# The convolutions of a state-space mixer: the first tap on ScalarE, and the engines' steps set one unit apart

## The chip, the cores and the metric

The kernel runs on one core of one Trainium2 chip. The metric is the device time of an execution in microseconds (us). TensorE (PE) multiplies, VectorE (DVE) and ScalarE (ACT) work element by element, GpSimd (POOL) helps them, and SyncE (SP) issues the loads of the weights. The engines run side by side and meet at semaphores.

## The reference, cut to what matters

Three layers work on x (256 tokens, 1024 features): attention and a gated feed-forward, a spatial gating unit and a gated feed-forward, and a third block whose mixer is half state-space scan, half attention. The change lies in that mixer's projections:

```python
proj = rmsnorm(x, norm_mix_pre) @ w_in              # z, xbc, dt, q, k, v
def depthwise_conv_centred(u, w, b):                # five taps over the tokens, 1536 channels
    out = conv(u, w, padding=[(2, 2)], feature_group_count=c)
    return out + b
xbc = silu(depthwise_conv_centred(xbc, conv_w, conv_b))
xs, B, C = split(xbc)                               # 1024, 256 and 256 channels
dt = softplus(dt_raw + dt_bias)                     # then the chunked scan, forwards and backwards
```

## The kernel before, in words

All weights come in units of 128 x 1024 fp32, in the order of their use, through a ring of six places (`RING`). For each unit n, SP loads `raw`, ScalarE writes the high half (`hi_of`, L144: a copy rounded to fp32r), VectorE the low half (`lo_of`, L149: raw minus high), and TensorE makes three products for each piece (`three`, L166 to L168): high by high, high by low, low by high. The high half of n waits until TensorE has used unit n-6, the load of n+6 until VectorE has split n. `hi_to` and `lo_to` split all units up to a number that haven't been split yet; where they stand in an engine's program is where the engine does it. Each engine takes its own instructions strictly in the written order.

The mixer's projections run in 12 steps j (`XT`), written out by hand for each engine. Unit `x_unit(j)` holds 128 channels of xbc; for j below 10 (`QKT`) the unit behind it holds 128 channels of q or k; steps 10 and 11 have the first unit alone. The result has channels on partitions and tokens along the row, so a convolution is five shifted multiply-adds along the row.

TensorE (`mixer_in_pe`, L1187): 24 matmuls of the x unit into bank 4 or 5, in turn; the two transposes of channel block j-1 (`turn`, L1193), which wait for its Silu; the 24 matmuls of the query or key unit into bank 2 or 3, which wait until VectorE has emptied that bank of block j-2. In step 0 it also makes the row of the norm and the transposes of dt, and waits for VectorE's copy of the row; in step 8 it makes the sums of dt (L1316).

VectorE (`mixer_in_dve`, L1248): the low splits up to `x_unit(j) + 5`; the copy of the x unit's result into `pad`, scaled by the row (L1263); the first tap with its bias (L1267, `tensor_scalar`); four more taps (L1271, `scalar_tensor_tensor`, each waits for the one before); in steps 0 and 1 small operations of dt; the low split of `x_unit(j) + 6`; the query or key of the same step (L1281).

ScalarE (`mixer_in_act`, L1225): the high split up to `x_unit(j) + 5`; the copy of the transposed block j-2 out of PSUM (`move`, L1229); the high split of `x_unit(j) + 6`; the Silu of block j (L1245), which waits for its last tap. In step 0 it works on dt between these (Exp, a table load, Ln, a table load for Silu). Behind the loop it loads the table of Exp and makes the decays (L1330).

`pad` and `S_CV` (the running sum) have two places each, used in turn. Behind the loop comes the scan (`ssd_pe`, `ssd_act`, `ssd_dve`, `ssd_pool`). TensorE enters it once move 9, copy 11 and the last key are done. POOL makes masks for it (L1399), two ahead at first and then as TensorE uses them. VectorE's first product for it (L1514, `decayed`) waits for the decays, and ScalarE's exponentials for Silu 11.

Of the kernel before, what the change touches and what calls it, by code (L numbers as in the profile page):

```python
# [9 lines left out]
ACT = mybir.ActivationFunctionType  # L10
ALU = mybir.AluOpType
# [3 lines left out]
SEQ = 256  # L15
# [5 lines left out]
HEADS, KV_HEADS, DH = 16, 4, 64  # L21
REP = HEADS // KV_HEADS
QT = HEADS * DH // P
KVT = KV_HEADS * DH // P
QKT = QT + KVT
# [9 lines left out]
XT = 1536 // P  # L35
# [29 lines left out]
C_XBC = C_CONV + 2 * FT * 4  # L65
# [14 lines left out]
def build(nc, w, x_in, cols_in, misc_in, tables_in, rows_in, ws_in, wdt_in, out):  # L80
# [3 lines left out]
    def sem(name):  # L84
        return nc.alloc_semaphore(name)

    def signals(prefix, names):

        return namedtuple(prefix, names)(*(sem(f"{prefix}_{name}") for name in names.split()))
# [9 lines left out]
    cols = sb("cols", [P, COLS])  # L99
# [7 lines left out]
    pad = sb("pad", [P, 2, SEQ + 4])  # L107
    arena = sb("arena", [P, 16640])
    ps = nc.alloc_psum_tensor("ps", [P, 8, 512], F32)
# [19 lines left out]
    unit_used = sem("unit_used")  # L129
# [29 lines left out]
    def lo_to(dve, n):  # L159
        while dve_at[0] <= min(n, UNITS - 1):  # L160
            lo_of(dve, dve_at[0])
            dve_at[0] += 1
# [59 lines left out]
    ROW = cut(16384, SEQ)  # L222
# [361 lines left out]
    A_Q, A_K, A_V = cut(3072, QT, SEQ), cut(5120, KVT, SEQ), cut(5632, TT, KV_HEADS * DH)  # L584
# [585 lines left out]
    S_E, S_LA, S_CB = cut(12288, 4, 512), cut(14336, 2, 512), cut(15360, 2, 2, P)  # L1170
    S_CV, S_SL = cut(12288, 2, SEQ), cut(12800, 2, SEQ)
    S_Z = cut(12288, TT, D)
    x_sem = signals("xbc", "copied conv silu turned moved")

    def xbc_dst(j):
        return S_SL[:, j % 2, :] if j < 8 else S_F[:, j - 8, :]


    def x_unit(j):
        return N_MIX + 2 + (2 * j if j < QKT else j + QKT)  # L1180

    def x_bank(j):
        return 4 + j % 2
# [3 lines left out]
    def mixer_in_pe(pe, u, q):  # L1187
        def turn(j):
            pe.wait_ge(x_sem.silu, j + 1)
            if j >= 2:  # L1190
                pe.wait_ge(x_sem.moved, j - 1)
            for tt in range(TT):
                mm = pe.transpose(ps[:, 6 + j % 2, tt * P:(tt + 1) * P],  # L1193
                                  xbc_dst(j)[:, tt * P:(tt + 1) * P], ident)
            mm.then_inc(x_sem.turned, 1)

        def v(tt, pre):
            for h in range(2):
                tokens(pe, N_MIX + h, [ps[:, b, 0:256] for b in V_BANKS], 4 * h, 4, 256, pre=pre, tiles=(tt,))

        v(0, Pre(u.next.lo, 2 * KT * u.n))
        turn_tile_pe(pe, u, 1)
        v(1, after(u))
        dt_pe(pe)
        for j in range(XT):
            if j >= 2:
                pe.wait_ge(x_sem.copied, j - 1)
            features(pe, x_unit(j), ps[:, x_bank(j), 0:SEQ])
            if j == 0:
                row_pe(pe, u, 2)  # L1210
                dt_turn_pe(pe)
            if 1 <= j < XT - 1:
                turn(j - 1)
            if j == DT_SUMS:
                dt_sums_pe(pe)
            if j < QKT:
                if j == 0:
                    pe.wait_ge(next_sems.row_out, 4)
                elif j == 1:
                    pe.wait_ge(q.v, TT)  # L1220
                else:
                    pe.wait_ge(q.qk, j - 1)
                features(pe, x_unit(j) + 1, ps[:, 2 + j % 2, 0:SEQ])

    def mixer_in_act(act):  # L1225
        def move(j):
            act.wait_ge(x_sem.turned, j + 1)
            dst = S_X[:, :, j * P:(j + 1) * P] if j < 8 else S_B[:, :, (j - 8) * P:(j - 7) * P]
            act.activation(dst, ps[:, 6 + j % 2, 0:SEQ].rearrange("p (a b) -> p a b", a=TT),  # L1229
                           ACT.Copy).then_inc(x_sem.moved, 1)  # L1230

        for j in range(XT):
            if j == 0:
                dt_move_act(act)
            hi_to(act, x_unit(j) + 5)
            if 2 <= j < XT:
                move(j - 2)
            hi_to(act, x_unit(j) + 6)
            if j == 0:
                dt_act(act)  # L1240
                act.preload_act_table(ACT.Silu)
            act.wait_ge(x_sem.conv, 5 * j + 5)
            if 2 <= j < 8:
                act.wait_ge(x_sem.turned, j - 1)
            act.activation(xbc_dst(j), S_CV[:, j % 2, :], ACT.Silu).then_inc(x_sem.silu, 1)  # L1245
        decay_act(act)

    def mixer_in_dve(dve, q, u):  # L1248
        dve.wait_ge(next_sems.inv, TT * (u.n + 1))
        for tt in range(TT):  # L1250
            dve.wait_ge(unit_used, N_MIX + 2)
            dve.tensor_scalar(A_V[:, tt, :], ps[:, V_BANKS[tt], 0:256], st[:, 14 + tt:15 + tt], None,
                              ALU.mult).then_inc(q.v, 1)
        dt_before, dt_between, dt_behind = dt_dve(dve)
        for j in range(XT):
            lo_to(dve, x_unit(j) + 5)
            if j == 0:
                row_dve(dve, 4, 2)
                dt_before()
            c = C_XBC + 6 * j  # L1260
            b = j % 2
            dve.wait_ge(unit_used, x_unit(j) + 1)
            dve.tensor_tensor(pad[:, b, 2:2 + SEQ], ps[:, x_bank(j), 0:SEQ], ROW, ALU.mult).then_inc(x_sem.copied, 1)  # L1263
            dve.wait_ge(x_sem.copied, j + 1)
            if j >= 2:
                dve.wait_ge(x_sem.silu, j - 1)
            dve.tensor_scalar(S_CV[:, b, :], pad[:, b, 0:SEQ], cols[:, c:c + 1], cols[:, c + 5:c + 6],  # L1267
                              ALU.mult, ALU.add).then_inc(x_sem.conv, 1)
            for k in range(1, 5):
                dve.wait_ge(x_sem.conv, 5 * j + k)  # L1270
                dve.scalar_tensor_tensor(S_CV[:, b, :], pad[:, b, k:k + SEQ], cols[:, c + k:c + k + 1],  # L1271
                                         S_CV[:, b, :], ALU.mult, ALU.add).then_inc(x_sem.conv, 1)
            if j == 0:
                dt_between()
            if j == 1:
                dt_behind()
            lo_to(dve, x_unit(j) + 6)
            if j < QKT:
                dve.wait_ge(unit_used, x_unit(j) + 2)
                dst = A_Q[:, j, :] if j < QT else A_K[:, j - QT, :]  # L1280
                dve.scalar_tensor_tensor(dst, ps[:, 2 + j % 2, 0:SEQ], DH ** -0.5 if j < QT else 1.0, ROW,  # L1281
                                         ALU.mult, ALU.mult).then_inc(q.qk, 1)


    dts = sb("dts", [P, 12, 64])
# [46 lines left out]
    def dt_dve(dve):  # L1332


        v = lambda k: dts[:, k, :]
        two = lambda k: v(k).rearrange("p (a b) -> p a b", a=TT)
        row32 = lambda t, o: t[:, o:o + 32].rearrange("p (a b) -> p a b", a=1).to_broadcast([P, TT, 32])
        step = [0]

        def then(ins):  # L1340
            ins.then_inc(d_sem.step, 1)
            step[0] += 1
            dve.wait_ge(d_sem.step, step[0])

        def before():
            dve.wait_ge(d_sem.turned, 1)
            for tt in range(TT):
                then(dve.scalar_tensor_tensor(two(V_A)[:, tt, :], ps[:, 1, SEQ + 32 * tt:SEQ + 32 * (tt + 1)],
                                              st[:, 14 + tt:15 + tt], misc[:, M_DTB:M_DTB + 32], ALU.mult, ALU.add))
            then(dve.scalar_tensor_tensor(v(V_NEG), v(V_A), -1.0, v(V_A), ALU.mult, ALU.min))  # L1350

        def between():
            dve.wait_ge(d_sem.exp, 2)
            then(dve.tensor_scalar(v(V_U), v(V_E), 1.0, None, ALU.add))
            then(dve.tensor_scalar(v(V_D), v(V_U), 1.0, None, ALU.subtract))
            then(dve.tensor_scalar(v(V_EQ), v(V_U), 1.0, None, ALU.is_equal))
            then(dve.tensor_tensor(v(V_D2), v(V_D), v(V_EQ), ALU.add))
            then(dve.reciprocal(v(V_RD), v(V_D2)))
            then(dve.tensor_tensor(v(V_T), v(V_E), v(V_RD), ALU.mult))

        def behind():
            dve.wait_ge(d_sem.ln, 1)
            then(dve.tensor_tensor(v(V_D), v(V_L), v(V_EQ), ALU.add))
            then(dve.tensor_tensor(v(V_T), v(V_T), v(V_D), ALU.mult))
            then(dve.scalar_tensor_tensor(v(V_DT), v(V_A), 0.0, v(V_T), ALU.max, ALU.add))
            then(dve.scalar_tensor_tensor(two(V_DA), two(V_DT), -1.0, row32(ea, 0), ALU.mult, ALU.mult))

        return before, between, behind
# [381 lines left out]
    first, mix = Norm(0, *pre_sems), Norm(1, *pre_sems)  # L1750
# [264 lines left out]
```

## Time and profile before

| | us |
|---|---|
| median of 3 runs | 1149.39 (1148.82 to 1149.48) |
| the profiled execution | 1150.9 |
| its span, first to last instruction | 1149.1 |
| TensorE busy in it | 1088.8 (95%) |
| VectorE busy | 818.2 (71%) |
| ScalarE busy | 609.1 (53%) |
| POOL busy | 128.2 (11%) |
| mean granted clock of TensorE | 0.986 |

The profile is of one execution, and its times are counted from its first instruction. Matmuls are pipelined, so a busy TensorE is not one at its peak. The granted clock is a share of 2.4 GHz. The loop of the mixer's projections lies between about 721 and 800 us of the span, the scan behind it until about 850.

### The profile page before, as it was taken

The numbers are of one execution on the slowest core, as the hardware profiler recorded it, in microseconds if no ns is written. First come the engines' busy times: TensorE is split into PE (matmuls) and PEld (weight loads), VectorE is DVE, ScalarE is ACT, GpSimd is POOL, SyncE is SP. The second block draws the span as 40 slices with busy tenths as digits, with TensorE's granted clock in tenths as the row PEclk, the third lists the DMA queues.
The fourth block names the chain that finished last, engine by engine and source line by source line (L and its number), as shares of the span: only waits on it lengthen the run. The fifth ranks groups of instructions, "written<-read, shape, count | busy, mean of one in ns | idle before, by whom it ended". The sixth has DMA issues, their size and how long they took to land.

```text
span 1149.1 us, 20549 instructions
## 1 busy us (share of the span) xinstructions
PE 1088.8 (95%) x7226; PEld 983.5 (86%) x7226; DVE 818.2 (71%) x1282; ACT 609.1 (53%) x1046; POOL 128.2 (11%) x139
## 2 busy tenths in 40 slices
PE   7989999999999999999999999897788898999997
PEld 7878999999788997779999998897666687999996
DVE  6757877776744567878777776899878658666664
ACT  6657444444755846656444446544337746444442
POOL 0140111111010012201111110101402200000000
PEclk9999999999999999999999999899899999999999
DMA  8253665565455555435656563554001273655540
GB/s 331 95 190 133 216 194 189 189 195 183 163 204 165 191 177 175 155 111 165 201 183 198 185 201 110 184 183 148 1 1 37 93 229 119 201 185 190 190 147 37
DMA packets 51381, 185.08 MB, mean 161 GB/s; under 512 B 5728, under 2 KB 6240, under 8 KB 51328
## 3 DMA queue, kind: packets, MB, share of 16 engines
q1 hardware_dynamic: 49248, 178.28, 47.2%
q0 software_dynamic: 1504, 5.44, 1.4%
q8 instruction: 35, 0.57, 0.2%
q10 hardware_dynamic: 576, 0.64, 0.2%
q14 instruction: 18, 0.15, 0.0%
HBM read 183.28 MB, written 1.05 MB: 160 GB/s over the span
## 4 chain that ended last, share of the span: by engine, by line
PE 85%; DVE 9%; ACT 4%; issue 2%; DMA 0%; DVEq 0%; SPq 0%; ACTq 0%
PE ps L208 26%; PE ps L166 17%; PE ps L167 17%; PE ps L168 17%; DVE w_lo L149 2%; DVE arena L1534 1%; PE ps L645 1%; PE ps L674 1%; ACT arena L698 1%; DVE a_lo L382 1%; DVE x L400 1%; PE ps L658 1%; DVE arena L393 1%; ACT a_hi L376 1%; PE ps L1444 1%
## 5 line engine op out<-in xcount | busy, mean ns | idle before, releaser
L149 DVE TENSOR_TENSOR w_lo<-raw,w_hi 128x1024 fp32r<-128x1024 f32 x336 | 420.9, 1262 | 140.5 <-ACT w_hi L144 140.3
L144 ACT ACTIVATE w_hi<-raw 128x1024 fp32r<-128x1024 f32 x336 | 347.1, 1052 | 174.1 <-PE ps L168 106.7
L166 PE MATMUL ps<-a_hi,w_hi 128*128 128x256 f32 x1408 | 401.6, 285 | 3.4 <-DVE arena L354 3.0
L167 PE MATMUL ps<-a_lo,w_hi 128*128 128x256 f32 x1408 | 399.6, 284 | 0.0
L168 PE MATMUL ps<-a_hi,w_lo 128*128 128x256 f32 x1408 | 399.5, 284 | 0.0
L166 PEld LDWEIGHTS ps<-a_hi,w_hi 128*128 128x128 f32 x1408 | 271.2, 193 | 7.7 <-DVE arena L354 3.1
L167 PEld LDWEIGHTS ps<-a_lo,w_hi 128*128 128x128 f32 x1408 | 271.3, 193 | 2.5
L168 PEld LDWEIGHTS ps<-a_hi,w_lo 128*128 128x128 f32 x1408 | 271.2, 193 | 0.0
L208 PE MATMUL ps<-w_hi,a_hi 128*128 128x512 f32 x496 | 158.1, 400 | 8.3 <-DVE a_lo L1116 3.0
L208 PE MATMUL ps<-w_lo,a_hi 128*128 128x512 f32 x496 | 153.5, 390 | 0.0
L208 PE MATMUL ps<-w_hi,a_lo 128*128 128x512 f32 x496 | 153.3, 390 | 0.0
L208 PEld LDWEIGHTS ps<-w_lo,a_hi 128*128 128x128 f32 x496 | 93.1, 188 | 20.6
L208 PEld LDWEIGHTS ps<-w_hi,a_lo 128*128 128x128 f32 x496 | 93.1, 188 | 20.1
L208 PEld LDWEIGHTS ps<-w_hi,a_hi 128*128 128x128 f32 x496 | 86.0, 190 | 24.8 <-DVE w_lo L149 4.5
L524 POOL TENSOR_TENSOR arena<-arena 128x256 f32<-128x256 f32 x44 | 47.1, 1070 | 308.8 <-ACT arena L511 308.8
L511 ACT ACTIVATE arena<-arena 128x256 f32<-128x256 f32 x44 | 18.4, 419 | 101.8 <-DVE arena L551 101.8
L166 PE MATMUL ps<-w_hi,a_hi 128*128 128x512 f32 (+1 forms) x160 | 60.6, 379 | 0.0
L516 ACT ACTIVATE a_hi<-arena 128x256 fp32r<-128x256 f32 x44 | 18.4, 418 | 77.9 <-DVE arena L557 77.9
L167 PE MATMUL ps<-w_lo,a_hi 128*128 128x512 f32 (+1 forms) x160 | 59.0, 369 | 0.0
L168 PE MATMUL ps<-w_hi,a_lo 128*128 128x512 f32 (+1 forms) x160 | 58.9, 368 | 0.0
L551 DVE SCALAR_TENSOR_TENSOR arena<-pad,cols,arena 128x256 f32<-128x256 f32 x88 | 42.7, 485 | 10.2 <-DVE arena L547 0.3
L166 PEld LDWEIGHTS ps<-w_hi,a_hi 128*128 128x128 f32 x160 | 30.1, 188 | 7.6 <-issue 2.2
(183 smaller groups left out, 1064.6 us busy)
## 6 DMA issues: line engine op xcount, KB each, us to landing
raw<-in_w SPq DMA_DIRECT2D x336, 512.0 KB, 4.2
row<-in_rows POOLq DMA_DIRECT2D x7, 512.0 KB, 4.0
x<-in_x SPq DMA_DIRECT2D x2, 512.0 KB, 4.8
out<-x SPq DMA_DIRECT2D x4, 256.0 KB, 2.0
misc<-in_misc POOLq DMA_DIRECT2D x1, 512.0 KB, 6.1
arena<-in_ws POOLq DMA_DIRECT2D x1, 512.0 KB, 7.5
tab<-in_tables POOLq DMA_DIRECT2D x1, 320.0 KB, 4.8
tab<-in_tables POOLq DMA_DIRECT2D x1, 256.0 KB, 5.1
```

The costliest lines, as they stand in the source:

```text
L144: act.activation(w_hi[:, s, :], raw[:, s, :], ACT.Copy).then_inc(hi_done, 1)
L149: dve.tensor_tensor(w_lo[:, s, :], raw[:, s, :], w_hi[:, s, :].bitcast(F32), ALU.subtract).then_inc(lo_done, 1)
L166: pe.matmul(o, l_hi, r_hi, start=first, stop=False)
L167: pe.matmul(o, l_hi, r_lo, start=False, stop=False)
L168: return pe.matmul(o, l_lo, r_hi, start=False, stop=last)
L208: mm = pe.matmul(ps[:, 2 * tt + c, :], a[:, slot, t], b[:, s, c * 512:(c + 1) * 512], start=f, stop=z)
L376: act.activation(a_hi[:, k, tile(tt)], spun(tt, k), ACT.Copy, scale=gain(g, k)).then_inc(u.next.hi, 1)
L382: dve.scalar_tensor_tensor(a_lo[:, k, tile(tt)], spun(tt, k), gain(g, k), a_hi[:, k, tile(tt)].bitcast(F32), ALU.mult, ALU.subtract).then_ ...
L511: act.activation(F_GL[:, b, :], F_CV[:, b, :], ACT.Gelu_apprx_tanh).then_inc(f.gelu, 1)
L516: act.activation(a_hi[:, f_slot(t), :], F_PR[:, b, :], ACT.Copy).then_inc(f.hi, 1)
L524: pool.tensor_tensor(F_GR[:, b, :], F_GL[:, b, :], ROW, ALU.mult).then_inc(f.scaled, 1)
L551: dve.scalar_tensor_tensor(F_CV[:, b, :], pad[:, b, k:k + SEQ], col(k), F_CV[:, b, :], ALU.mult, ALU.add).then_inc(f.conv, 1)
```

## The change

VectorE's first tap with its bias becomes an Identity activation on ScalarE (`first_tap`), with the tap's column as scale and the bias column as bias. It waits for VectorE's copy and for the Silu that last read its place. VectorE's taps wait for it.

The order of all three programs moves. TensorE's transposes of block j-2 (was j-1) stand in step j. ScalarE does in step j: the high split of `x_unit(j) + 5`, move j-3 (was j-2), the first tap of j, the high split of `x_unit(j) + 6`, and the Silu of j-1 (was j); move 9 and Silu 11 stand behind the loop. VectorE does in step j: the low split of `x_unit(j) + 5`, the copy of j (with two more waits, on the taps and the first tap that read this place of `pad`), the low split of `x_unit(j) + 6`, the query or key of j-1 (was j, at the end), the four taps of j, and then the small operations of dt in steps 0 and 1.

```diff
--- before.py
+++ after.py
@@ -1170,7 +1170,7 @@
     S_E, S_LA, S_CB = cut(12288, 4, 512), cut(14336, 2, 512), cut(15360, 2, 2, P)
     S_CV, S_SL = cut(12288, 2, SEQ), cut(12800, 2, SEQ)
     S_Z = cut(12288, TT, D)
-    x_sem = signals("xbc", "copied conv silu turned moved")
+    x_sem = signals("xbc", "copied first conv silu turned moved")
 
     def xbc_dst(j):
         return S_SL[:, j % 2, :] if j < 8 else S_F[:, j - 8, :]
@@ -1209,8 +1209,8 @@
             if j == 0:
                 row_pe(pe, u, 2)
                 dt_turn_pe(pe)
-            if 1 <= j < XT - 1:
-                turn(j - 1)
+            if 2 <= j < XT:
+                turn(j - 2)
             if j == DT_SUMS:
                 dt_sums_pe(pe)
             if j < QKT:
@@ -1229,20 +1229,35 @@
             act.activation(dst, ps[:, 6 + j % 2, 0:SEQ].rearrange("p (a b) -> p a b", a=TT),
                            ACT.Copy).then_inc(x_sem.moved, 1)
 
+        def first_tap(j):
+            c = C_XBC + 6 * j
+            act.wait_ge(x_sem.copied, j + 1)
+            if j >= 2:
+                act.wait_ge(x_sem.silu, j - 1)
+            act.activation(S_CV[:, j % 2, :], pad[:, j % 2, 0:SEQ], ACT.Identity, bias=cols[:, c + 5:c + 6],
+                           scale=cols[:, c:c + 1]).then_inc(x_sem.first, 1)
+
+        def silu(j):
+            act.wait_ge(x_sem.conv, 4 * j + 4)
+            if 2 <= j < 8:
+                act.wait_ge(x_sem.turned, j - 1)
+            act.activation(xbc_dst(j), S_CV[:, j % 2, :], ACT.Silu).then_inc(x_sem.silu, 1)
+
         for j in range(XT):
             if j == 0:
                 dt_move_act(act)
             hi_to(act, x_unit(j) + 5)
-            if 2 <= j < XT:
-                move(j - 2)
+            if 3 <= j < XT:
+                move(j - 3)
+            first_tap(j)
             hi_to(act, x_unit(j) + 6)
             if j == 0:
                 dt_act(act)
                 act.preload_act_table(ACT.Silu)
-            act.wait_ge(x_sem.conv, 5 * j + 5)
-            if 2 <= j < 8:
-                act.wait_ge(x_sem.turned, j - 1)
-            act.activation(xbc_dst(j), S_CV[:, j % 2, :], ACT.Silu).then_inc(x_sem.silu, 1)
+            else:
+                silu(j - 1)
+        move(XT - 3)
+        silu(XT - 1)
         decay_act(act)
 
     def mixer_in_dve(dve, q, u):
@@ -1251,6 +1266,12 @@
             dve.wait_ge(unit_used, N_MIX + 2)
             dve.tensor_scalar(A_V[:, tt, :], ps[:, V_BANKS[tt], 0:256], st[:, 14 + tt:15 + tt], None,
                               ALU.mult).then_inc(q.v, 1)
+        def query(j):
+            dve.wait_ge(unit_used, x_unit(j) + 2)
+            dst = A_Q[:, j, :] if j < QT else A_K[:, j - QT, :]
+            dve.scalar_tensor_tensor(dst, ps[:, 2 + j % 2, 0:SEQ], DH ** -0.5 if j < QT else 1.0, ROW,
+                                     ALU.mult, ALU.mult).then_inc(q.qk, 1)
+
         dt_before, dt_between, dt_behind = dt_dve(dve)
         for j in range(XT):
             lo_to(dve, x_unit(j) + 5)
@@ -1260,26 +1281,23 @@
             c = C_XBC + 6 * j
             b = j % 2
             dve.wait_ge(unit_used, x_unit(j) + 1)
+            if j >= 2:
+                dve.wait_ge(x_sem.conv, 4 * j - 4)
+                dve.wait_ge(x_sem.first, j - 1)
             dve.tensor_tensor(pad[:, b, 2:2 + SEQ], ps[:, x_bank(j), 0:SEQ], ROW, ALU.mult).then_inc(x_sem.copied, 1)
-            dve.wait_ge(x_sem.copied, j + 1)
-            if j >= 2:
-                dve.wait_ge(x_sem.silu, j - 1)
-            dve.tensor_scalar(S_CV[:, b, :], pad[:, b, 0:SEQ], cols[:, c:c + 1], cols[:, c + 5:c + 6],
-                              ALU.mult, ALU.add).then_inc(x_sem.conv, 1)
+            lo_to(dve, x_unit(j) + 6)
+            if 1 <= j <= QKT:
+                query(j - 1)
+            dve.wait_ge(x_sem.first, j + 1)
             for k in range(1, 5):
-                dve.wait_ge(x_sem.conv, 5 * j + k)
+                if k > 1:
+                    dve.wait_ge(x_sem.conv, 4 * j + k - 1)
                 dve.scalar_tensor_tensor(S_CV[:, b, :], pad[:, b, k:k + SEQ], cols[:, c + k:c + k + 1],
                                          S_CV[:, b, :], ALU.mult, ALU.add).then_inc(x_sem.conv, 1)
             if j == 0:
                 dt_between()
             if j == 1:
                 dt_behind()
-            lo_to(dve, x_unit(j) + 6)
-            if j < QKT:
-                dve.wait_ge(unit_used, x_unit(j) + 2)
-                dst = A_Q[:, j, :] if j < QT else A_K[:, j - QT, :]
-                dve.scalar_tensor_tensor(dst, ps[:, 2 + j % 2, 0:SEQ], DH ** -0.5 if j < QT else 1.0, ROW,
-                                         ALU.mult, ALU.mult).then_inc(q.qk, 1)
 
 
     dts = sb("dts", [P, 12, 64])
```

## Rows read from the trace of the kernel before

**Rows 1.** Stretch table: busy us and instructions by engine, TensorE's clock, DMA share, GB/s

```profile
772.00:778.00 6.00, 6.00 (x52) 6.00 (x51) 5.45 (x9) 2.70 (x4) 0.00 (x0) 1.00 0.54 176
```

**Rows 2.** Timeline of TensorE in the loop: start us, us, engine, line, operation

```profile
784.88 0.38 PE L1193 MATMUL ps<-tab,arena 128*128 128x128 f32 x2
...
790.85 0.38 PE L1193 MATMUL ps<-tab,arena 128*128 128x128 f32 x2
```

**Rows 3.** Timeline of VectorE, one step of the loop and the next low split

```profile
785.08 0.42 DVE L1263 TENSOR_TENSOR pad<-ps,arena 128x256 f32<-128x256 f32 x1 [0.50 <-PE ps L168]
785.54 0.41 DVE L1267 TENSOR_SCALAR arena<-pad,cols 128x256 f32<-128x256 f32 x1
785.99 2.05 DVE L1271 SCALAR_TENSOR_TENSOR arena<-pad,cols,arena 128x256 f32<-128x256 f32 x4
787.96 1.22 DVE L149 TENSOR_TENSOR w_lo<-raw,w_hi 128x1024 fp32r<-128x1024 f32 x1
789.09 0.42 DVE L1281 SCALAR_TENSOR_TENSOR arena<-ps,arena 128x256 f32<-128x256 f32 x1
789.47 1.22 DVE L149 TENSOR_TENSOR w_lo<-raw,w_hi 128x1024 fp32r<-128x1024 f32 x1
...
793.92 1.22 DVE L149 TENSOR_TENSOR w_lo<-raw,w_hi 128x1024 fp32r<-128x1024 f32 x1
```

**Rows 4.** Timeline of TensorE at the start: in brackets the idle before

```profile
727.71 0.58 PE L166 MATMUL ps<-a_hi,w_hi 128*128 128x256 f32 x1 [2.98 <-DVE arena L354]
```

**Rows 5.** Stretch table, behind that wait

```profile
728.00:736.00 8.00, 8.00 (x47) 8.00 (x47) 7.41 (x17) 4.57 (x7) 0.00 (x0) 0.64 0.44 168
```

**Rows 6.** Timeline of VectorE at the end of the loop

```profile
795.06 0.42 DVE L1263 TENSOR_TENSOR pad<-ps,arena 128x256 f32<-128x256 f32 x1
...
795.96 3.55 DVE L1271 SCALAR_TENSOR_TENSOR arena<-pad,cols,arena 128x256 f32<-128x256 f32 x4
...
801.53 0.17 DVE L1514 TENSOR_TENSOR decayed<-dts,ex 128x8 f32<-128x8 f32 x1
```

**Rows 7.** Groups of ScalarE by form: count, busy us, mean ns, idle before

```profile
L144 ACT ACTIVATE w_hi<-raw 128x1024 fp32r<-128x1024 f32 x336 | 347.1, 1052 | 174.1 <-PE ps L168 106.7 <-PE ps L208 64.3 <-DMA raw<-in_w 2.7
...
L1015 ACT ACTIVATE arena<-arena,lns 128x128 f32 x36 | 15.6, 480 | 0.0
```

**Rows 8.** Timeline of ScalarE: start of the loop, and one later step

```profile
728.91 1.28 ACT L1324 ACT_TABLE_LOAD   x1
...
788.07 0.42 ACT L1245 ACTIVATE arena<-arena 128x256 f32<-128x256 f32 x1 [1.87 <-DVE arena L1271]
788.39 1.04 ACT L144 ACTIVATE w_hi<-raw 128x1024 fp32r<-128x1024 f32 x1
789.35 0.36 ACT L1229 ACTIVATE arena<-ps 128x256 f32<-128x256 f32 x1
```

**Rows 9.** Timeline of VectorE in the first two steps

```profile
728.52 0.42 DVE L1263 TENSOR_TENSOR pad<-ps,arena 128x256 f32<-128x256 f32 x1
...
731.39 0.19 DVE L1354 TENSOR_SCALAR dts<-dts 128x64 f32<-128x64 f32 x1
...
736.39 0.43 DVE L1263 TENSOR_TENSOR pad<-ps,arena 128x256 f32<-128x256 f32 x1 [0.52 <-PE ps L168]
...
739.26 0.22 DVE L1363 TENSOR_TENSOR dts<-dts 128x64 f32<-128x64 f32 x1
...
740.29 1.23 DVE L149 TENSOR_TENSOR w_lo<-raw,w_hi 128x1024 fp32r<-128x1024 f32 x1
```

**Rows 10.** Timelines of TensorE and POOL at the start of the scan

```profile
795.57 0.46 PE L1424 MATMUL ps<-arena 128*128 128x128 f32 x2 [1.47 <-ACT arena L1229]
...
797.01 2.22 POOL L1399 TENSOR_TENSOR arena<-tab,dts 128x512 f32<-128x512 f32 x2 [52.61 <-PE ps L1414]
```

**Rows 11.** Stretch table, in the spatial gating unit

```profile
432.00:440.00 8.00, 6.58 (x35) 5.43 (x33) 5.18 (x7) 5.95 (x12) 0.92 (x2) 1.00 0.73 238
```

## The prediction

> **What bounds the kernel now.** I read the stretch table first, then the timelines of VectorE, TensorE and ScalarE in the loop of the mixer convolutions, then the same timelines at its end. From 772 to 778 us TensorE is busy 6.00 of 6.00 us while VectorE has 5.45 and ScalarE 2.70 [rows 1]. So in the loop TensorE sets the pace: its two transposes of a step recur after 790.85 - 784.88 = 5.97 us [rows 2]. A step is 48 matmuls and these transposes.
>
> VectorE is only just faster. From start to next start [rows 3]: copy 0.46, first tap 0.45 (785.54 to 785.99), four taps 1.97 (785.99 to 787.96), low split 1.13 (787.96 to 789.09), query 0.38 (789.09 to 789.47), second low split 1.14 (793.92 to 795.06). The sum is 5.53 us, 0.44 under TensorE's 5.97. The copy at 785.08 waited 0.50 us for a matmul [rows 3]: VectorE is ready before its work is.
>
> Two places are not TensorE's. At the start it waits 2.98 us for the row copied by VectorE and then runs at a granted clock of 0.64 over 728 to 736 us, mostly the lower level of 1.2 GHz [rows 4, 5]; the change leaves what is in front of this wait alone. At the end the chain runs through VectorE: copy 11 at 795.06, taps until 795.96 + 3.55 = 799.51, then Silu, a table load and the decays on ScalarE, and VectorE's decayed at 801.53 [rows 6]. The state product of the scan waits for that.
>
> **The change, part by part.** *Removed from VectorE:* twelve first taps, 0.45 us of its order each, 5.4 us in all. In the loop they lie beside TensorE's work and are worth nothing there; only the last is on the path, 0.45.
>
> *Added to ScalarE:* twelve Identity activations of 128x256 with a column for scale and one for bias. The nearest row is Identity with two such columns on 128x128, 0.480 us. A plain activation takes 0.42 for 256 elements and 1.052 for 1024, so 128 more cost (1.052 - 0.42) / 6 = 0.105; I take 0.585 [rows 7, 8]. Bounds: 0.42, the plain one of the same size, and 0.70, both columns dearer on the longer tile. ScalarE is busy 2.70 of 6 us [rows 1], so as work this is free. The Trainium skill ("ScalarE: Activation LUTs", rules for kernel authors) says to keep multiplies and adds on VectorE; the comparison here, 0.585 against 0.41, agrees, and by busy time alone the rule would cost nothing in this loop.
>
> *The new exchange* is what costs. In a step VectorE now does the copy, then the low split of unit x+6, the lagging query, the taps, and the low split of the next x+5. But that low split of x+6 needs ScalarE's high split of x+6, and ScalarE issues it behind first tap j, which waits for VectorE's copy j. Before, VectorE ran five taps between copy and split (0.45 + 1.97 = 2.42 us), long enough for ScalarE to have the split ready. Now nothing stands there. From the copy's start to the low split's start:
> - the copy 0.42, and 0.03 until ScalarE starts (taps end 785.99 + 2.05 = 788.04, Silu starts 788.07): 0.45 [rows 3, 8]
> - first tap 0.585, of which the next activation overlaps 0.10 (788.07 + 0.42 against 788.39): 0.49 [rows 8]
> - high split 1.052 and 0.03 back to VectorE: 1.08 [rows 7]
>
> together 2.02 us, of which VectorE works 0.42. Then low split 1.13, query 0.38, taps 1.97, low split 1.14: 4.62. The step closes on itself because the engine takes its instructions in order: 6.64 us, against TensorE's 5.97. The first tap gone saves 0.45; the idle 1.56 more than eats it.
>
> *When TensorE feels it.* The unit of query j waits for query j-2 to leave its bank, and that query now stands one step later. It is done 2.02 + 1.13 + 0.42 + 0.03 = 3.6 us after the copy of its step. The start uses up the slack:
> - copy 0 stays at 728.52 [rows 9]. ScalarE's tap and high split end at 730.54, low split to 731.67, taps to 733.64, the first dt operation 0.19 later [rows 9]. Only then can ScalarE do its Ln (about 0.3, as the Exps) and load Silu's table (1.28 [rows 8]): 735.4. Its next high split is done at 736.5, VectorE's low split at 737.6: copy 1 at 737.6 instead of 736.39 [rows 9].
> - copy 2 one ring later plus the last dt operations, 740.29 - 739.26 = 1.03 [rows 9]: 737.6 + 6.64 + 1.03 = 745.3. Query 1 is out at 748.9. TensorE, done with x unit 1 at 736.4 (copy 1 of before waited for it), would be done with x unit 3 at 736.4 + 2 x 5.97 = 748.3 and want that bank. It pauses 0.5 us, and from here about 6.64 - 5.97 = 0.67 us in each step.
> - copies 3 to 10: 8 x 6.64 = 53.1, so copy 10 at 798.4. Copy 11 has no low split in front: 5.50 later, 803.9. Before it was 795.06 [rows 6]: 8.8 us later.
>
> *The end of the loop.* Before, the taps of 11 ended 799.51 - 795.06 = 4.45 us after the copy, slowed to 3.55 from 2.05 while POOL worked from 797.01, 1.44 after TensorE's first scan product [rows 3, 6, 10]. Now they begin 2.02 + 1.13 = 3.15 after the copy. The scan's first product waits for move 9, which stands behind Silu 10 and the high split: 0.45 + 0.49 + 0.96 + 0.32 + 0.36 = 2.6 after the copy [rows 8]; POOL starts at 4.0 or, at the low clock, nearer 5. So one tap or two are slowed: 2.80, between 2.05 and 3.55. The end is 5.95 after the copy, 1.5 us more than now. The low split that stood behind the taps has gone in front of them, and that is most of it. What follows (Silu, table, decays) is the same 2.0 us.
>
> *Moved at no cost:* transposes one step later (their Silu ends 0.45 + 0.49 + 0.96 + 0.42 = 2.3 us after the copy [rows 8], and TensorE asks a step after it, 6.64), moves one step later, the waits on pad's reuse, which guard work three instructions back, and SP's loads of weights, which follow the low splits and are needed three steps on. If the cover went, the transpose would wait next, in the same step and for the same exchange.
>
> **Sum:** 8.8 + 1.5 = +10.3 us. The scan behind the loop is a chain of single products between VectorE and ScalarE, with TensorE idle in it, so nothing gives this back. The profiled execution took 1150.9 us (span 1149.1), so 1161.2 on its scale; it stands 1.5 above the median of 1149.4, so I forecast 1159.7. In this case: tap at 0.42, 11 x -0.17 = -1.8, and the end unslowed, -0.75: 1157.2. Tap at 0.70, +1.3, both last taps slowed, +0.75, the three more waits at 0.1 us a step, +1.1: 1162.9.
>
> **Rivals.** *TensorE keeps the pace.* If the exchange is shorter by 0.67 us or the splits run ahead of it, TensorE never pauses; copy 11 comes 0.7 earlier than now (it is then not held by a low split), the end costs 1.5: +0.8, 1150.2. For it: the busy sums, 5.08 for VectorE and 3.3 for ScalarE in 5.97. Against: the order in both programs and the 1.06 us of a high split. That one engine would be a unit ahead is what the change says; only TensorE and the Silu get that distance, copy and first tap stay in one step. Chance 0.06.
>
> *Faster: VectorE is the real bound.* Were VectorE's order the limit throughout, 12 x 0.45 = 5.4 us would go: 1144.0. For it: VectorE is at 5.53 of 5.97, and the end is its own. It decides from a VectorE step above 5.97. Against: TensorE has no gap in the loop [rows 1]. Chance 0.03.
>
> *Much slower: the clock.* TensorE now pauses in every step. In this trace the clock fell behind one pause of 2.98 us [rows 4, 5]; it stayed at 1.00 in a stretch with 6.58 of 8 us busy [rows 11], and here it would be busy 5.97 of 6.64. At 1.2 GHz a step would take up to twice 5.97 = 11.9 instead of 6.64, over eight steps some 42 us, a third of it if it only falls at times: 1159.7 + 14 = 1174 and up. The Trainium skill ("TensorE: Matmul & The Clock Gate", second failure mode) tells of a kernel whose short pauses between groups of matmuls kept throwing the clock back; by that rule this rival would hold, and [rows 11] speaks against it. Chance 0.03.
>
> **How the numbers follow.** Forecast case 0.88, 1157.2 to 1162.9; the rivals 0.06, 0.03, 0.03. The range is widened on both sides for steps of the start that I may have put too late or too early (one ring less or half a ring more): 1154 to 1164. A measurement of this kernel tells about 0.2%, 2.3 us, from no change. Faster 0.03, same 0.06, slower 0.91.
>
> **What would show it.** Right: VectorE idle about 1.6 us between each copy and the low split behind it, released by ScalarE's high split; copies 6.6 us apart from copy 2 on; TensorE's units of queries waiting 0.7 us for VectorE's query; clock near 1.00; copy 11 near 804. The first tap at 0.58. Wrong: copies still 5.97 apart, or a first tap with a table load of its own.

## The result and the profile after

The changed kernel takes 1160.01 us (median of 4 runs, 1159.31 to 1161.27) against 1149.43 for the kernel before (4 runs): 1.0095 times as long, 95% interval 1.0083 to 1.0108. It is 10.6 us slower; 10.3 were forecast.

The profiled execution took 1160.08 us with a span of 1158.3, only 9.2 more than the profiled span of before. The two profiles differ early, too: the granted clock from 60 to 120 us was 0.97 in the profile of before and 1.00 in this one, and copy 0 of the loop stands at 726.62 instead of 728.52, 1.9 us earlier. From copy 0 to the last instruction it is 431.7 us against 420.6, 11.1 more. So I compare distances from copy 0 and not times of the span.

VectorE's timeline of the changed kernel, with copy 0, one later step, and the end of the loop:

```profile
726.62 0.42 DVE L1287 TENSOR_TENSOR pad<-ps,arena 128x256 f32<-128x256 f32 x1
728.66 1.22 DVE L149 TENSOR_TENSOR w_lo<-raw,w_hi 128x1024 fp32r<-128x1024 f32 x1 [1.61 <-ACT w_hi L144]
...
735.86 0.42 DVE L1287 TENSOR_TENSOR pad<-ps,arena 128x256 f32<-128x256 f32 x1
...
783.12 0.42 DVE L1287 TENSOR_TENSOR pad<-ps,arena 128x256 f32<-128x256 f32 x1
785.16 1.23 DVE L149 TENSOR_TENSOR w_lo<-raw,w_hi 128x1024 fp32r<-128x1024 f32 x1 [1.62 <-ACT w_hi L144]
786.30 0.42 DVE L1272 SCALAR_TENSOR_TENSOR arena<-ps,arena 128x256 f32<-128x256 f32 x1
786.63 2.04 DVE L1295 SCALAR_TENSOR_TENSOR arena<-pad,cols,arena 128x256 f32<-128x256 f32 x4
788.59 1.22 DVE L149 TENSOR_TENSOR w_lo<-raw,w_hi 128x1024 fp32r<-128x1024 f32 x1
789.73 0.42 DVE L1287 TENSOR_TENSOR pad<-ps,arena 128x256 f32<-128x256 f32 x1
...
801.80 0.42 DVE L1287 TENSOR_TENSOR pad<-ps,arena 128x256 f32<-128x256 f32 x1
803.83 1.22 DVE L149 TENSOR_TENSOR w_lo<-raw,w_hi 128x1024 fp32r<-128x1024 f32 x1 [1.61 <-ACT w_hi L144]
804.97 2.04 DVE L1295 SCALAR_TENSOR_TENSOR arena<-pad,cols,arena 128x256 f32<-128x256 f32 x4
809.03 0.45 DVE L1532 TENSOR_TENSOR decayed<-dts,ex 128x8 f32<-128x8 f32 x1 [2.02 <-ACT ex L1348]
809.51 1.49 DVE L1537 TENSOR_TENSOR arena<-arena,decayed 128x512 f32<-128x512 f32 x1
```

The copy at 783.12 ends at 783.54 and VectorE then stands for 1.62 us until ScalarE's high split releases the low split (in brackets). From that copy to the next are 6.61 us, where [rows 2] and the copies of before had 5.97. ScalarE in the same step:

```profile
783.57 0.60 ACT L1237 ACTIVATE arena<-pad,cols 128x256 f32<-128x256 f32 x1 [3.53 <-DVE pad L1287]
784.08 1.04 ACT L144 ACTIVATE w_hi<-raw 128x1024 fp32r<-128x1024 f32 x1
785.03 0.40 ACT L1244 ACTIVATE arena<-arena 128x256 f32<-128x256 f32 x1
785.33 1.04 ACT L144 ACTIVATE w_hi<-raw 128x1024 fp32r<-128x1024 f32 x1
```

The round can be walked: the copy ends at 783.54, the tap starts at 783.57, the high split at 784.08 ends at 785.12, the low split starts at 785.16. ScalarE itself stood 3.53 us in front of the tap: it has time in plenty and is only asked too late. Who waited for whom, from 720 to 820 us (total, times, longest):

```profile
ACT arena L1237 <- DVE pad L1287: 42.5, 12, 4.8
...
DVE w_lo L149 <- ACT w_hi L144: 20.6, 13, 1.6
...
PEld ps L166 <- DVE arena L1272: 4.3, 7, 1.1
...
PE ps L166 <- DVE arena L354: 3.0, 1, 3.0
```

VectorE's thirteen waits for the high split make 20.6 us; TensorE's weight loads stood 4.3 us in seven waits for a query (L1272). In the trace of before no matmul and no weight load waited for anything from 729 to 792 us. The stretch table shows what that leaves of TensorE:

```profile
745.00:785.00 40.00, 37.34 (x303) 35.95 (x302) 29.27 (x48) 18.80 (x31) 0.48 (x1) 1.00 0.46 159
...
800.00:806.00 6.00, 1.58 (x7) 1.58 (x8) 4.21 (x8) 2.12 (x4) 0.00 (x0) 0.59 0.25 87
806.00:812.00 6.00, 3.28 (x15) 2.57 (x14) 3.87 (x9) 2.90 (x5) 3.08 (x3) 0.78 0.27 87
```

37.34 of 40 us busy, at a clock of 1.00. At the end of the loop the clock is 0.59, while TensorE waits for move 9. Its timeline there (in brackets the idle before):

```profile
798.69 0.44 PE L1193 MATMUL ps<-tab,arena 128*128 128x128 f32 x2 [2.80 <-ACT arena L1244]
804.42 0.80 PE L1442 MATMUL ps<-arena 128*128 128x128 f32 x2 [5.29 <-ACT arena L1229]
```

### The profile page after: what moved, and what is told of

It reads as the page before. It is cut to its first block, busy times and chain, and to the rows that moved or that the text cites. A ratio compares the mean times of both kernels' runs of the same rounds, so it can differ in the third digit from the quotient of the medians.

```text
span 1158.3 us, 20559 instructions
## 1 busy us (share of the span) xinstructions
PE 1090.2 (94%) x7226; PEld 982.7 (85%) x7226; DVE 809.7 (70%) x1270; ACT 613.7 (53%) x1058; POOL 126.6 (11%) x139
## 4 chain that ended last, share of the span: by engine, by line
PE 78%; DVE 14%; ACT 5%; issue 3%; DMA 0%; DVEq 0%; ACTq 0%; SPq 0%
PE ps L208 26%; PE ps L166 16%; PE ps L168 15%; PE ps L167 15%; DVE w_lo L149 5%; DVE arena L1552 2%; DVE arena L1295 2%; ACT w_hi L144 1%; PE ps L645 1%; DVE a_lo L382 1%; PE ps L674 1%; DVE x L400 1%; DVE arena L393 1%; PE ps L658 1%; ACT a_hi L376 1%
## 5 line engine op out<-in xcount | busy, mean ns | idle before, releaser
L208 PEld LDWEIGHTS ps<-w_lo,a_hi 128*128 128x128 f32 x496 | 93.1, 188 | 20.6
```

The lines of the kernel that those rows point to most:

```text
L208: mm = pe.matmul(ps[:, 2 * tt + c, :], a[:, slot, t], b[:, s, c * 512:(c + 1) * 512], start=f, stop=z)
```

## The experiments

Three theories were held against each other. The exchange: the high split stands behind the first tap and so behind VectorE's copy, and VectorE needs it next. The tap: a tap on ScalarE, with its two handovers, costs the step by itself. The query: letting the query out a step later stops TensorE.

**One part undone or done alone.** *The high split in front of the tap:*

```diff
-            first_tap(j)
             hi_to(act, x_unit(j) + 6)
+            first_tap(j)
```

> The changed kernel, but ScalarE makes the high split of unit x+6 in front of the first tap. Exchange theory (the split stands behind tap and copy): the idle of 1.62 us before VectorE's low split falls to 0.6 or less, copies 5.97 us apart, copy 11 some 7.5 to 8.5 us earlier than in the changed kernel, 1149 to 1150 us. Tap theory (a tap on ScalarE costs the step by itself): still 1158 to 1161. Query theory (the query let out a step later stops TensorE): still 1158 to 1161, with the waits of the query's unit for VectorE as they are.

Measured: 1149.70 us, 0.9995 times before (0.9982 to 1.0008). The whole loss is gone with two lines exchanged. Two copies of it in VectorE's timeline, with the low split behind the second:

```profile
785.04 0.43 DVE L1287 TENSOR_TENSOR pad<-ps,arena 128x256 f32<-128x256 f32 x1 [0.50 <-PE ps L168]
...
791.03 0.42 DVE L1287 TENSOR_TENSOR pad<-ps,arena 128x256 f32<-128x256 f32 x1 [0.18 <-PE ps L168]
792.18 1.23 DVE L149 TENSOR_TENSOR w_lo<-raw,w_hi 128x1024 fp32r<-128x1024 f32 x1 [0.73 <-ACT w_hi L144]
```

The copies are 5.99 us apart and wait for a matmul again; the wait for the high split is down to 0.73 us, where 0.6 or less was expected. Earlier in the loop, where VectorE still catches up from the start, its copies stand 5.10 us apart (749.17 and 754.27), against 5.53 before (749.21 and 754.74).

*The low split behind the taps*, with ScalarE as in the change:

```diff
             dve.tensor_tensor(pad[:, b, 2:2 + SEQ], ...).then_inc(x_sem.copied, 1)
-            lo_to(dve, x_unit(j) + 6)
             if 1 <= j <= QKT:
                 query(j - 1)
...
                 dt_behind()
+            lo_to(dve, x_unit(j) + 6)
```

> The changed kernel, but VectorE makes the low split of unit x+6 behind the taps, as before the change. Exchange theory: VectorE's step is copy, query, a wait of some 0.2 us for the tap, taps, two splits = 5.3 us, so TensorE sets 5.97 again: 1148.5 to 1150 us. Tap theory and query theory: still 1158 to 1161.

Measured: 1148.36 us, 0.9989 (0.9980 to 0.9999). The tap is still in front of the high split, but VectorE no longer meets that split behind it. What it waits for now is the tap itself, 4.7 us in twelve steps, so 0.4 a step where 0.2 was expected, and 0.7 at most (its waits, total, times, longest):

```profile
DVE arena L1294 <- ACT arena L1237: 4.7, 12, 0.7
```

The median is a little under that of before, and the traces say where: the way to copy 11 is the same, but `decayed` comes 5.16 us after it instead of 6.47 (table below). With the transposes and moves a step later POOL starts only at 799.87, when the taps of 11 (2.05 us) are done.

*The tap on ScalarE alone*, in the order of before:

```diff
+            act.wait_ge(x_sem.copied, j + 1)
...
+            act.activation(S_CV[:, j % 2, :], pad[:, j % 2, 0:SEQ], ACT.Identity, bias=..., scale=...
+                           ).then_inc(x_sem.first, 1)
             hi_to(act, x_unit(j) + 6)
...
-            dve.tensor_scalar(S_CV[:, b, :], pad[:, b, 0:SEQ], ...).then_inc(x_sem.conv, 1)
+            dve.wait_ge(x_sem.first, j + 1)
```

> The kernel before, with the first tap on ScalarE (between move and the high split of unit x+6) and nothing else moved. Exchange theory: VectorE waits 0.6 us for the tap, then taps and both splits, 5.7 us a step, under 5.97: 1149 to 1150.5 us. Tap theory: most of the loss is here, 1156 to 1161. Query theory: no loss, 1149 to 1150.

Measured: 1150.20 us, 1.0004 (0.9995 to 1.0014). The tap theory wanted most of the loss here. It falls. The handovers do cost VectorE something: it waits 0.67 us for each tap, and where it still catches up its copies stand 5.71 us apart (742.40 and 748.11) against 5.53 before. But 5.71 is under TensorE's 5.97, so it stays covered.

*The new order alone*, with the tap on VectorE:

```diff
-            first_tap(j)
             hi_to(act, x_unit(j) + 6)
...
+            dve.tensor_scalar(S_CV[:, b, :], pad[:, b, 0:SEQ], ...).then_inc(x_sem.conv, 1)
             lo_to(dve, x_unit(j) + 6)
-            dve.wait_ge(x_sem.first, j + 1)
```

> The order of the changed kernel on all three engines, with the first tap back on VectorE right behind the copy. Exchange theory: the high split no longer waits for the copy, so it is ready 1.1 us after the unit and VectorE has 0.9 us of copy and tap to do meanwhile: 1148.5 to 1150.5 us. Tap theory: no loss, 1149 to 1150. Query theory: the loss is here, 1156 to 1161.

Measured: 1151.97 us, 1.0021 (1.0007 to 1.0035): 2.4 us, more than the exchange theory gave and far less than the query theory. Copy 0 to copy 11 takes 65.78 us (727.43 to 793.21), 66.54 before, so the loop lost nothing. The end lost something: the taps of 11 stand behind the low split, and POOL, let go early by TensorE, works through all four of them. VectorE's timeline of it:

```profile
793.21 0.42 DVE L1285 TENSOR_TENSOR pad<-ps,arena 128x256 f32<-128x256 f32 x1
...
795.13 4.08 DVE L1296 SCALAR_TENSOR_TENSOR arena<-pad,cols,arena 128x256 f32<-128x256 f32 x4
801.23 0.17 DVE L1533 TENSOR_TENSOR decayed<-dts,ex 128x8 f32<-128x8 f32 x1 [2.02 <-ACT ex L1349]
```

and POOL's:

```profile
795.53 2.22 POOL L1418 TENSOR_TENSOR arena<-tab,dts 128x512 f32<-128x512 f32 x2 [51.71 <-PE ps L1433]
```

The taps take 4.08 us instead of 2.05, and `decayed` comes 8.02 us after copy 11 instead of 6.47. From copy 0 to `decayed` that is 0.8 us more than before. The rest of the 2.4 is not settled: in the profile the first three rounds of the scan behind it took 38.6 us (`decayed` at 801.23 and 839.81) against 36.2 (801.53 and 837.72), at a granted clock of 0.81 against 0.89 from 800 to 860 us. But e7_before_row_early, further down, had 38.3 us at 0.83 there and was no slower than before. The ten times fall into two groups, five from 1148.2 to 1150.7 and five from 1153.3 to 1154.8, with the median in the gap; the profile, at 1154.13, is of the upper one. The mean of the lower group, 1149.9, is 0.6 us over the median of before, about what the traces show up to `decayed`. What makes the upper group is open.

So the tap alone costs nothing that can be told, the order alone 2.4 us (0.8 to 4.0, in two groups of times), and both together 10.6.

**The suspected price doubled.** *Each first tap made twice*, the first time into a place that nobody reads:

```diff
+            act.activation(junk[:, 512:768], pad[:, j % 2, 0:SEQ], ACT.Identity, bias=..., scale=...)
             act.activation(S_CV[:, j % 2, :], pad[:, j % 2, 0:SEQ], ACT.Identity, bias=..., scale=...
```

> The changed kernel with each first tap made twice on ScalarE, the first time into a place that nobody reads: 0.50 us more of ScalarE in front of the high split in each of 12 steps. Exchange theory: it is in the closed round of every step, so the copies stand 7.1 us apart instead of 6.60 and the time grows by 11 to 12 x 0.50 = 5.5 to 6: 1165 to 1166.5 us. Rival (ScalarE, busy under half of the step, has room for it): 1160 to 1161.

Measured: 1166.83 us, 1.0153 (1.0136 to 1.0169), against 1.0095 for the change: 0.0058, 6.7 us more, and 0.3 us above the expected range. In VectorE's timeline the copies stand 7.10 apart and the wait is 2.11 us:

```profile
787.31 0.42 DVE L1289 TENSOR_TENSOR pad<-ps,arena 128x256 f32<-128x256 f32 x1
...
794.41 0.42 DVE L1289 TENSOR_TENSOR pad<-ps,arena 128x256 f32<-128x256 f32 x1
796.94 1.23 DVE L149 TENSOR_TENSOR w_lo<-raw,w_hi 128x1024 fp32r<-128x1024 f32 x1 [2.11 <-ACT w_hi L144]
```

ScalarE was busy in 21.38 of the 40 us from 745 on, and yet each half microsecond more of it counted in full: 75.18 us from copy 0 to copy 11 became 80.59, 5.4 more for 11 steps.

**The end of the loop.** *In the last step the taps in front of the low split*, the rest as changed:

```diff
-            lo_to(dve, x_unit(j) + 6)
+            if j < XT - 1:
+                lo_to(dve, x_unit(j) + 6)
```

(`lo_to(dve, N_Z + 5)` behind the loop makes up for it.)

> The changed kernel, but in the last step VectorE makes the taps in front of the low split instead of behind it. Exchange theory: the loop stays at 6.60 us a step and copy 11 where it is; the taps begin 1.1 us after the copy instead of 3.2, and may lose up to 1.5 us of the 2.1 to POOL: 0.6 to 2.1 us less, 1158 to 1159.5 us. Rival (the loss is at the end of the loop and not in it): 1150 to 1152.

Measured: 1158.03 us, 1.0069 (1.0052 to 1.0086): 2.6 thousandths under the change, with intervals that meet. VectorE's timeline:

```profile
803.64 0.42 DVE L1287 TENSOR_TENSOR pad<-ps,arena 128x256 f32<-128x256 f32 x1
804.73 2.05 DVE L1296 SCALAR_TENSOR_TENSOR arena<-pad,cols,arena 128x256 f32<-128x256 f32 x4 [0.67 <-ACT arena L1237]
...
808.79 0.17 DVE L1533 TENSOR_TENSOR decayed<-dts,ex 128x8 f32<-128x8 f32 x1 [0.88 <-ACT ex L1349]
```

Up to `decayed` the gain is 2.1 us: it comes 5.15 us after copy 11 instead of 7.23, with the copies 6.60 apart as in the change.

**Towards a version that beats both.** TensorE's wait of 2.98 us for the row [rows 4] comes from two low splits that VectorE makes in front of the row's copy (VectorE's timeline of before):

```profile
724.97 2.35 DVE L149 TENSOR_TENSOR w_lo<-raw,w_hi 128x1024 fp32r<-128x1024 f32 x2
727.23 0.42 DVE L354 COPY arena<-ps 128x256 f32<-128x256 f32 x1
```

*The row first, in the kernel before:*

```diff
-            lo_to(dve, x_unit(j) + 5)
             if j == 0:
                 row_dve(dve, 4, 2)
                 dt_before()
+            lo_to(dve, x_unit(j) + 5)
```

> The kernel before with the same early copy of the row and nothing else: the wait falls from 3.0 to 0.7 us, 1144.5 to 1147.5 us. It tells how much of the gain of the version with both edits has nothing to do with the first tap: all of it by the exchange theory.

Measured: 1149.96 us, 0.9996 (0.9986 to 1.0005). A miss. TensorE's timeline (idle in brackets) shows where the gain went:

```profile
724.97 0.38 PE L166 MATMUL ps<-a_hi,w_hi 128*128 128x256 f32 x1 [0.70 <-DVE arena L354]
...
733.18 0.69 PE L1193 MATMUL ps<-tab,arena 128*128 128x128 f32 x2 [2.20 <-ACT arena L1245]
```

The wait fell to 0.70 us, and the transposes of block 0 waited 2.20 us for Silu 0 instead. That Silu stands on ScalarE behind Ln, which waits for VectorE's small dt operations, and behind the table load:

```profile
731.15 0.26 ACT L1326 ACTIVATE dts<-dts 128x64 f32<-128x64 f32 x1 [3.11 <-DVE dts L1354]
731.42 1.28 ACT L1241 ACT_TABLE_LOAD   x1
732.71 0.42 ACT L1245 ACTIVATE arena<-arena 128x256 f32<-128x256 f32 x1
```

TensorE's clock was 0.82 from 728 to 736 us. What was won at one wait was mostly paid at the next: 1.0 us was left at copy 11 (table below), and that was not found in the time. *The same edit on the kernel with the high split first:*

> The kernel with the high split in front of the first tap, and in step 0 VectorE copies TensorE's row before the two low splits that stood in front of it. Both are now in the clear of the exchange; the wait of 3.0 us for the row falls to 0.7, and if TensorE's clock stays up behind it, another 2.6 us go: 1144.5 to 1147.5 us. If the splits behind the row are late for their units instead: 1149 to 1151.

Measured: 1146.05 us, 0.9968 (0.9955 to 0.9980). Here the transposes of block 0 stand a step later. TensorE's waits at the start of the loop, by its timeline:

```profile
724.39 0.39 PE L166 MATMUL ps<-a_hi,w_hi 128*128 128x256 f32 x1 [0.71 <-DVE arena L354]
...
736.41 0.44 PE L1193 MATMUL ps<-tab,arena 128*128 128x128 f32 x2 [0.24 <-ACT arena L1244]
...
743.38 0.38 PE L166 MATMUL ps<-a_hi,w_hi 128*128 128x256 f32 x1 [0.20 <-DVE arena L1272]
```

They are short, copy 11 comes 3.25 us earlier than before when counted from x unit 0 (table below), and the clock stays up, as the stretch table has it:

```profile
728.00:736.00 8.00, 8.00 (x69) 7.96 (x67) 6.53 (x14) 6.18 (x10) 0.00 (x0) 1.00 0.56 196
```

*The same edit on the kernel with the low split behind the taps:*

> The kernel with the low split behind the taps (e2_lo_behind) and the early copy of the row. In e7_before_row_early the wait for the row was gone, but TensorE's transposes of block 0 waited 2.2 us for Silu 0 instead; with the transposes a step later that wait is gone too. If the value lies in the later transposes, this gains as much as e6_split_first_row_early: 1144.5 to 1147 us. If it lies in the high split in front of the tap: 1149 to 1150.

Measured: 1145.86 us, 0.9973 (0.9963 to 0.9982). As good as e6_split_first_row_early, with the splits in another order; so the place of the high split is not what decides. The wait of the transposes is not quite gone, though: it was 1.06 us for block 0 and 1.03 for block 1. By the ratios the early row itself is worth 3.1 us on the order of e1_split_first (0.9995 to 0.9968, intervals apart) and 1.8 on that of e2_lo_behind (0.9989 to 0.9973, intervals that just meet). *And on the new order with the tap on VectorE:*

> The order of the changed kernel with the first tap on VectorE (e4_lag_alone) and the early copy of the row. If the later transposes alone make the early row worth something: 3 to 4 us less than e4_lag_alone, 1147 to 1149 us. If the tap on ScalarE is needed for it: as e4_lag_alone, 1150.5 to 1152.5.

Measured: 1149.79 us, 1.0005 (0.9995 to 1.0014), some 1.8 us better than e4_lag_alone by the ratios, with intervals that meet. That is between the two expectations. The transposes wait no more, but TensorE stood for queries 0 and 1:

```profile
737.39 0.38 PE L166 MATMUL ps<-a_hi,w_hi 128*128 128x256 f32 x1 [1.46 <-DVE arena L1271]
...
744.88 0.39 PE L166 MATMUL ps<-a_hi,w_hi 128*128 128x256 f32 x1 [1.26 <-DVE arena L1271]
```

VectorE, with 0.45 us of tap more in each step, had not caught up from the start, and the query is let out a step later than before. The change and e5_tap_twice, with the exchange, also wait for queries; of the orders without it this is the only one in which a matmul waited more than 0.2 us for one.

For all kernels, from TensorE's start on x unit 0 (720.91 before) to copy 11, and from copy 11 to `decayed`, in us:

| kernel | x unit 0 to copy 11 | to decayed | ratio to before |
|---|---|---|---|
| before | 74.15 | 6.47 | |
| the change | 82.78 | 7.23 | 1.0095 |
| e1_split_first | 74.54 | 5.53 | 0.9995 |
| e2_lo_behind | 74.21 | 5.16 | 0.9989 |
| e3_tap_alone | 73.33 | 6.47 | 1.0004 |
| e4_lag_alone | 73.38 | 8.02 | 1.0021 |
| e5_tap_twice | 88.20 | 7.72 | 1.0153 |
| e8_tail | 82.77 | 5.15 | 1.0069 |
| e7_before_row_early | 73.13 | 6.47 | 0.9996 |
| e6_split_first_row_early | 70.90 | 5.52 | 0.9968 |
| e9_lo_behind_row_early | 71.72 | 5.15 | 0.9973 |
| e10_lag_row_early | 72.88 | 6.63 | 1.0005 |

These are single executions, and the clock at the start of the loop differs among them (from 728 to 736 us it was 0.64 before, 0.79 in e3_tap_alone and 0.91 in the change). So differences of a microsecond in the first column are not argued from.

## Why the prediction was right

- *The closed round.* Predicted 6.64 us, measured 6.60 to 6.61. Its terms: copy to low split 2.02 against 2.04 (783.12 to 785.16); the four parts behind it 4.62 against 4.57. That the order is the cause is shown from both sides: exchange two lines and it is gone (e1_split_first), put 0.50 more into it and each step takes it up (e5_tap_twice).
- *First tap.* Predicted 0.585 us, measured 0.60. The Trainium skill ("ScalarE: Activation LUTs", what ACT_TABLE_LOAD costs) gives 186 ns and 0.833 for each element, and 93 for each pointer operand. For 256 elements and two such operands that is an estimate of 585 ns, and 600 was measured. No table load came with Identity: the loop has its two of step 0, as before.
- *The start.* Copy 1 predicted 9.1 us after copy 0, measured 9.24 (726.62 to 735.86); copy 11 75.4, measured 75.18; 8.8 us more than before, measured 8.64.
- *The end: the one term that was off.* Move 9 let the scan's first product start 2.62 us after copy 11, as predicted (2.6). But I had the taps of 11 end 5.95 us after the copy, with one or two slowed by POOL; they ended 5.21 after it, none slowed (2.04 us), because POOL started only then, at 807.01. So `decayed` came 0.76 us later after copy 11 than before (7.23 against 6.47), not 1.5. That is half of the predicted term. POOL met what comes next: `decayed` took 0.45 us instead of 0.17 [rows 6], and the product behind it 1.49 where 0.69 stood before (801.73, the same timeline as [rows 6]), 1.1 us that I hadn't counted. Added up, 8.6 + 0.76 + 1.1 = 10.5 against a measured 10.6. But that these 1.1 us last is argued, not shown: three rounds of the scan took 37.9 us (`decayed` at 809.03 and 846.92) against 36.2 before, 1.7 more, while in e1_split_first they took 36.7 with a product of 1.49 us too. The loop's part, 8.6, stood by itself; that the sum came within 0.3 us is partly luck, as what the end was short of came back in the scan, for which I had put nothing.
- *The removed taps were worth nothing in the loop:* once VectorE has caught up, TensorE sets the pace whenever the exchange is out (e1_split_first: copies at 5.99).
- *Rival, TensorE keeps the pace:* it fell with the 4.3 us of waits for queries. Its own condition, that the splits run ahead of the exchange, is e1_split_first, and there the time is near what it said (1149.7 against 1150.2). Its terms were not: from x unit 0 copy 11 came 0.4 us later than before and not 0.7 earlier, and the end was 0.9 us shorter and not 1.5 longer.
- *Rival, VectorE the real bound:* fell. In e1_split_first VectorE's own step was shorter by the 0.43 us of the tap (5.10 against 5.53) and the time stayed. (e3_tap_alone can't tell: there it won 0.45 and waited 0.67.)
- *Rival, the clock:* fell. Over 745 to 785 us TensorE paused 2.66 us in all and the granted clock stayed at 1.00. The Trainium skill ("TensorE: Matmul & The Clock Gate", second failure mode) tells of a kernel in which short pauses between groups of matmuls threw it back; in this loop they did not. It was lower at the start, behind the wait of 2.98 us that before has too (0.91 from 728 to 736 us), and at the end of the loop (0.59), around waits of 2.80 and 5.29 us.

What is open: I have not separated how much of the gain of e6_split_first_row_early comes from the shorter wait itself and how much from the clock that stays up behind it; both appear together in e6_split_first_row_early, e9_lo_behind_row_early and e10_lag_row_early (clock 1.00 from 728 to 736 us), and in e7_before_row_early, where the wait was short and the clock fell, another wait came in. Open are also the two groups of times of e4_lag_alone, and how much of the change's 10.6 us lies in the scan's rounds.

## What to carry to other kernels

Work moved to an idle engine is free only where the program order around it allows it. Before moving it, write out for each engine what stands behind the new wait, and look whether the other engine needs one of those things next: two engines that each stand behind the other once in a step make a round as long as all the work on the way through both, however idle they are. The remedy need not be to undo the move; here it was to issue the independent split first. And when a wait is taken away and nothing is gained, read the next wait: the early row was worth 0.5 us, within the noise, in the order of before, and 1.8 to 3.1 us in the orders in which the transposes came a step later.

## What the runs showed of the hardware that was not expected

- Who is slowed by POOL depends on a microsecond. VectorE's four taps (128x256) took 2.04 us alone, 3.55 in the kernel before and 4.08 in e4_lag_alone while POOL's 128x512 products ran; the 128x512 product of `decayed` took 0.69 us alone and 1.49 beside POOL. In the change the taps were out of POOL's way and the product was in it. In e2_lo_behind both ran clear (2.05 and 0.69).
- One more activation in ScalarE's queue costs less than its duration: 0.60 us busy, 0.50 in the step, because the next one starts 0.09 to 0.10 us before it ends (783.57 + 0.60 = 784.17 against 784.08).
